# One tile of the second output projection interleaved with the last pair of stick-breaking heads, and four remainders computed on GpSimd

## The chip, the cores and the metric

One core of one Trainium2 chip runs the whole program. The metric is the device time of one execution in microseconds. The kernel before takes 3147.85 us, the median of three runs that lie between 3146.23 and 3148.41 us.

## What is computed

The program is two transformer blocks on 1024 positions of width 1024. What matters here is the attention part of the second block:

```
q, k, v, q_mem = split(x @ w_in_sb_2)                # 12 heads of 64 columns, and 4 memory heads
for each block of 128 queries:                       # stick-breaking attention
    z        = q_b @ k_b^T / 8
    log_stay = where(strict, log_sigmoid(-z), 0)
    later    = reverse_cumsum(log_stay) - log_stay
    w        = where(strict, exp(log_sigmoid(z) + later), 0)
    out      = w @ v_b
y = concat(mix, mem_out) @ w_out_2                   # the second output projection, 1024 x 1024
x = layer_norm(ALPHA * x + y)
```

The 12 stick-breaking heads give 768 rows of the projection's input, which are the blocks k = 0 to 5 of 128 rows (two heads in each). The memory attention gives the blocks 6 and 7 and is done before the stick-breaking stage.

## The kernel before

Activations lie transposed, features on the partitions. A dense layer is a series of tiles: one tile makes 128 output rows by 1024 positions in PSUM (`dense`, two slots, the use number u chooses u % 2), from 8 blocks of 128 input rows. Precision comes from a split: a value is the sum of a rounded part (`_hi`) and a remainder (`_lo`). One block of a tile is therefore six matmuls of 512 columns (`product`, L517, L518, L521: hi by hi and hi by lo for the two halves of the positions, then lo by hi for the two halves).

**Weights.** SyncE streams raw weight tiles into a ring of two. GpSimd splits each: one addition of zero into `w_hi` (L426), one subtraction into `w_lo` (L428), again a ring of two. The split of tile t waits until tile t - 2 is done (`pool.wait_ge(tile_done, t - 1)`), and a tile's first matmul waits for `weights_split`. In the stick-breaking stage GpSimd does the same work in four parts of 512 columns (`split_part`, L459 and L466), one part for a step, at the steps listed in `SPLIT_W`.

**The stick-breaking stage** is written out by hand in 144 steps: 12 for a head, 24 for a pair of heads, numbered n from 0. The last pair has steps 120 to 143. One step is a strip of 128 queries by up to 512 keys. In step n
- TensorE computes the scores of strip n (L934 to L936), transposes the weights of strip n - 6 (`turn_weights`, L946) and multiplies those of strip n - 8 by the values (`values`, L960 and L961); then it does two blocks of the next pair's projection, if `PROJECT` lists the step (the last one it lists is n = 125).
- ScalarE makes sigmoid(z) and sigmoid(-z) of strip n (L1378, L1384) and rounds the transposed weights of strip n - 6 (L1392). Its waits are for the scores and for `pv_done` of strip n - 7, less one.
- VectorE does the scan over strip n (L1935, preceded by a one-column product L1934 for the strips that go on from others, which are the last four of a head), then the remainder `wt_lo` of strip n - 6 (L1942), which reads PSUM. At n % 12 = 0 and 8 it also finishes a half head into `y2_f` (L1924; the page calls it y_f).
- GpSimd multiplies strip n by the scan (L476), then does its part of a weight split, if any.

TensorE starts the transposes of a step only when `w_split`, VectorE's remainder of two strips earlier, is there. So each engine runs ahead of the others by a step or so at most, and all work goes in the order in which it is written.

**The second output projection** has the tiles T_OUT2 (159) to T_OUT2 + 7. Its input blocks are taken in the order `Y2_ORDER` = 0, 1, 2, 3, 4, 6, 7, 5. Block 5 holds the last pair of heads and comes last. The first seven are made ready inside the stick-breaking loop: at the steps in `EARLY_AT`, which are n = 130, 132, ..., 142, ScalarE rounds `y2_f` into `a_hi` (L1406) and VectorE subtracts to make `a_lo` (the helper `low`, L1543). Block 5 follows after the loop. The weights of T_OUT2 are split at the steps 120 to 123, those of T_OUT2 + 1 at the steps 127 to 130.

After the loop TensorE waits for all heads (`y_copied`) and runs `two_tiles`: tile 0 and tile 1 of this projection together, tile 1 four blocks behind tile 0, so that tile 0 ends four blocks ahead of tile 1. Tile 0 uses slot 1 of `dense` (where the stick-breaking stage collects its outputs), tile 1 uses slot 0 (where it projects). The tiles 2 to 5 follow one by one, and `last_two` does the rest with the layer norm's sums. VectorE adds each tile to the residual (`add_mixed`, L1964) and adds up moments (L1481, L1471). ScalarE fetches the spilled residual from memory with two transfers that it issues once `y_copied` is complete (L1408, L1409).

Of the kernel before, what the change touches and what calls it, by code (L numbers as in the profile page):

```python
# [20 lines left out]
F32 = mybir.dt.float32  # L21
F32R = mybir.dt.float32r
ACT = mybir.ActivationFunctionType
ALU = mybir.AluOpType
# [5 lines left out]
KB = D // P  # L30
# [8 lines left out]
SB_H = 12  # L39
# [40 lines left out]
U_OUT2 = U_SB  # L80
# [53 lines left out]
           for c, a in enumerate((0, 7, 15)) for q in range(4) if p < SB_H // 2 or c < 2}  # L134
Y2_ORDER = (0, 1, 2, 3, 4, 6, 7, 5)
EARLY = 7
EARLY_AT = {PAIR_STEPS * (SB_H // 2 - 1) + 10 + 2 * j: j for j in range(EARLY)}


NORM_SPLIT = (None, 2, 0, 2, 4)  # L140
# [47 lines left out]
def build(nc, io, out):  # L188
    with ExitStack() as ctx:
# [5 lines left out]
        def sem(name):  # L195
            return ctx.enter_context(nc.semaphore(name))
# [69 lines left out]
        def par(name, k=0):  # L266
# [34 lines left out]
        parts = {n: (sem(n + "_rounded"), sem(n + "_split")) for n in (  # L301
            "h", "mem", "ym", "yc", "ya", "merged", "h2", "hidden", "x2", "mem2", "y2", "x3", "hidden2")}
        yc_ready = sem("conv_out_ready")

        turned, roped, turn_free = sem("proj_turned"), sem("proj_rotated"), pair("turn_free")
        idx_round, idx_split, stacked, stack_copied = (sem("index_rounded"), sem("index_split"), sem("index_stacked"),
# [116 lines left out]
        def _(pool):  # L423
# [48 lines left out]
            def stick_steps():  # L472
                for n in range(STICK_STEPS):
                    w, width = weights_of(n), chunk(n)[5]
                    pool.wait_ge(scanned, n + 1)
                    pool.tensor_tensor(w[:, 0:width - 1], w[:, 0:width - 1], stay[n % STRIPS][:, 1:width], ALU.mult  # L476
                                       ).then_inc(w_ready, 1)
                    if n in SPLIT_W:
                        t, part = SPLIT_W[n]
                        split_part(T_SB + t, part)  # L480

            split_tiles(RAW, T_ATT + 2)

# [17 lines left out]
        def _(pe):  # L501
# [467 lines left out]
            for n in range(STICK_STEPS + PV_LAG):  # L969
                if n < STICK_STEPS:  # L970
                    scores(n)
                if TURN_LAG <= n < STICK_STEPS + TURN_LAG:
                    turn_weights(n - TURN_LAG)
                if n >= PV_LAG:
                    values(n - PV_LAG)
                if n in PROJECT and PROJECT[n][0] < SB_H // 2:
                    p, c, half, b = PROJECT[n]
                    project(p, c, half, b, b + 2)
                if n in TURN_V:
                    turn_values(*TURN_V[n])  # L980

            pe.wait_ge(v_split, SB_H)
            pe.wait_ge(y_copied, 2 * SB_H)
            for n in range(KB):
                if n == 0:
                    two_tiles(T_OUT2, U_OUT2, parts["y2"][1], Y2_ORDER)
                elif 2 <= n < KB - 2:
                    tile(T_OUT2 + n, U_OUT2 + n)
            last_two(3, T_OUT2 + KB - 2, U_OUT2 + KB - 2, lambda h: moments(3, h, U_OUT2))
            repeat(pe, FF2_GROUPS - 1, feed(  # L990
                T_FF2, U_FF2, FG, parts["hidden2"][1], FG, (FF2_TILES, FF2_USES),
# [470 lines left out]
        def _(dve):  # L1462
# [455 lines left out]
            for n in range(STICK_STEPS + PV_LAG + 1):  # L1918
                e = n - PV_LAG - 1
                if e >= 0 and group_end(e) is not None:  # L1920

                    head, th = group_end(e) // 2, group_end(e) % 2
                    dve.wait_ge(low_ready, group_end(e) + 1)
                    dve.tensor_tensor(y2_f[HD * (head % 2):HD * (head % 2) + HD, head // 2, 512 * th:512 * th + 512],  # L1924
                                      out_bank(th)[0:HD, :], out_low[:, th, :], ALU.add).then_inc(y_copied, 1)
                if n < STICK_STEPS:
                    _, kind, _, _, _, width = chunk(n)
                    strip, before = stay[n % STRIPS], stay[(n - 4) % STRIPS]
                    dve.wait_ge(stay_ready, n + 1)
                    if kind == 2:  # L1930

                        dve.wait_ge(scanned, n - 3)
                        w = weights_of(n)
                        dve.tensor_tensor(w[:, 511:512], w[:, 511:512], before[:, 0:1], ALU.mult)  # L1934
                    dve.tensor_tensor_scan(strip[:, 0:width][:, ::-1], strip[:, 0:width][:, ::-1],  # L1935
                                           zero[:, 0:1].broadcast_to([P, width]), before[:, 0:1] if kind == 2 else 1.0,
                                           ALU.mult, ALU.add).then_inc(scanned, 1)
                m = n - TURN_LAG
                if 0 <= m < STICK_STEPS:
                    c0 = P * (3 - m % 4) if m % HEAD_STEPS < 8 else 0  # L1940
                    dve.wait_ge(w_round, m + 1)
                    dve.tensor_tensor(wt_lo[:, m % 2, c0:512], turn_bank(m, c0), wt_hi[:, m % 2, c0:512].bitcast(F32),  # L1942
                                      ALU.subtract).then_inc(w_split, 1)
                if n in TAKE_Q:
                    take_q(*TAKE_Q[n])
                if n in TAKE_K:
                    take_k(*TAKE_K[n])
                if n in SPLIT_V:
                    take_values(*SPLIT_V[n])
                if n in EARLY_AT:  # L1950
                    j = EARLY_AT[n]
                    k = Y2_ORDER[j]
                    low((a_hi[:, k, :], a_lo[:, k, :]), k, y2_f[:, k, :], "y2", j + 1)

            for j in range(EARLY, KB):
                k = Y2_ORDER[j]
# [272 lines left out]
```

## Time and profile before

| | us |
|---|---|
| median of three runs | 3147.85 |
| lowest and highest run | 3146.23, 3148.41 |
| the profiled execution's own time | 3153.3 |
| its span | 3151.5 |
| its mean granted TensorE clock | 0.96 of full speed |

The page gives for the span: PE 94% busy, weight loads 76%, VectorE 54%, ScalarE 25%, GpSimd 37%. In the page's table of 40 slices of 78.8 us, the last heads and the start of the projection lie in slices 29 and 30 (from 2206 us to 2364 us), where TensorE's digits are 7 and 9 and VectorE's 9 and 3. The granted clock is in tenths of full speed. Times below are microseconds from the start of the span; in the timelines the columns are start, duration, engine, line, operation, operands, and in brackets the idle time before with what ended it.

### The profile page before, as it was taken

The numbers are of one execution on the slowest core, as the hardware profiler recorded it, in microseconds if no ns is written. First come the engines' busy times: TensorE is split into PE (matmuls) and PEld (weight loads), VectorE is DVE, ScalarE is ACT, GpSimd is POOL, SyncE is SP. The second block draws the span as 40 slices with busy tenths as digits, with TensorE's granted clock in tenths as the row PEclk, the third lists the DMA queues.
The fourth block names the chain that finished last, engine by engine and source line by source line (L and its number), as shares of the span: only waits on it lengthen the run. The fifth ranks groups of instructions, "written<-read, shape, count | busy, mean of one in ns | idle before, by whom it ended". The sixth has DMA issues, their size and how long they took to land.

```text
span 3151.5 us, 35444 instructions
## 1 busy us (share of the span) xinstructions
PE 2962.3 (94%) x13362; PEld 2385.4 (76%) x13362; DVE 1690.4 (54%) x2322; ACT 781.9 (25%) x1429; POOL 1160.1 (37%) x649
## 2 busy tenths in 40 slices
PE   7987999998999899999999889999798999999997
PEld 4675878885777688888888668887675888888885
DVE  3475899985553533232332647888937333333327
ACT  4154011103531211011110355666613000000003
POOL 2330434441023334333443415555532433344331
PEclk9978999996999999999999999999898999999998
DMA  3110112221032111111111210000020111111111
GB/s 144 41 34 7 47 67 81 80 80 67 1 130 71 41 47 47 47 53 47 47 47 49 72 67 27 27 21 27 21 87 27 47 51 49 47 47 47 53 47 61
DMA packets 45054, 165.41 MB, mean 52 GB/s; under 512 B 4880, under 2 KB 6160, under 8 KB 43920
## 3 DMA queue, kind: packets, MB, share of 16 engines
q1 hardware_dynamic: 37168, 129.31, 12.4%
q10 hardware_dynamic: 7776, 34.61, 2.8%
q8 instruction: 72, 1.18, 0.2%
q14 instruction: 38, 0.31, 0.0%
HBM read 147.12 MB, written 16.78 MB: 52 GB/s over the span
## 4 chain that ended last, share of the span: by engine, by line
PE 82%; DVE 12%; ACT 2%; issue 2%; DVEq 1%; DMA 0%; POOL 0%; ACTq 0%; SPq 0%; POOLq 0%
PE dense L517 21%; PE dense L518 20%; PE dense L521 20%; DVE a_lo L1543 2%; DVE stay L1935 2%; PE dense L908 2%; PE side L813 2%; PE dense L909 2%; PE dense L910 2%; PE dense L557 1%; PE dense L823 1%; PE dense L558 1%; PE dense L559 1%; PE dense L740 1%; PE side L946 1%
## 5 line engine op out<-in xcount | busy, mean ns | idle before, releaser
L426 POOL TENSOR_TENSOR w_hi<-raw,zero 128x1024 fp32r<-128x1024 f32 x210 | 400.8, 1908 | 1572.2 <-PE dense L521 1300.2
L517 PE MATMUL dense<-a_hi,w_hi 128*128 128x512 f32 x2000 | 783.4, 392 | 14.1 <-DVE T L1681 5.6
L518 PE MATMUL dense<-a_lo,w_hi 128*128 128x512 f32 x2000 | 780.4, 390 | 0.0
L521 PE MATMUL dense<-a_hi,w_lo 128*128 128x512 f32 x2000 | 617.9, 390 | 0.0
L428 POOL TENSOR_TENSOR w_lo<-raw,w_hi 128x1024 fp32r<-128x1024 f32 x210 | 526.4, 2506 | 16.5
L517 PEld LDWEIGHTS dense<-a_hi,w_hi 128*128 128x128 f32 x2000 | 376.7, 188 | 95.7 <-issue 7.7
L521 PEld LDWEIGHTS dense<-a_hi,w_lo 128*128 128x128 f32 x2000 | 376.9, 188 | 78.9
L518 PEld LDWEIGHTS dense<-a_lo,w_hi 128*128 128x128 f32 x2000 | 376.7, 188 | 79.0 <-issue 1.2
L517 PE MATMUL dense<-b_hi,w_hi 128*128 128x512 f32 x832 | 327.2, 393 | 5.2 <-DVE T L1841 2.5
L518 PE MATMUL dense<-b_lo,w_hi 128*128 128x512 f32 x832 | 324.7, 390 | 0.0
L1821 DVE TENSOR_TENSOR x_res<-x_res,dense 128x1024 f32<-128x1024 f32 x100 | 122.1, 1221 | 329.6 <-PE dense L521 328.3
L1841 DVE SCALAR_TENSOR_TENSOR T<-dense,tiny,T 128x1023 f32<-128x1023 f32 x88 | 112.9, 1283 | 296.6 <-ACT T L1275 293.0
L521 PE MATMUL dense<-b_hi,w_lo 128*128 128x512 f32 x832 | 256.7, 390 | 0.0
L476 POOL TENSOR_TENSOR stick_weights<-stick_weights,stay 128x511 f32<-128x511 f32 (+2 forms) x144 | 132.1, 918 | 174.8 <-DVE stay L1935 174.8
L517 PEld LDWEIGHTS dense<-b_hi,w_hi 128*128 128x128 f32 x832 | 156.7, 188 | 45.8 <-issue 4.8
L1435 ACT ACTIVATE b_hi<-T 128x1024 fp32r<-128x1024 f32 x32 | 34.0, 1063 | 610.1 <-DVE T L2014 610.1
L521 PEld LDWEIGHTS dense<-b_hi,w_lo 128*128 128x128 f32 x832 | 156.5, 188 | 32.9
L518 PEld LDWEIGHTS dense<-b_lo,w_hi 128*128 128x128 f32 x832 | 156.8, 188 | 31.7
L1275 ACT ACTIVATE T<-dense,tiny 128x1024 f32<-128x1024 f32 x44 | 49.2, 1118 | 516.9 <-PE dense L521 511.1
L1646 DVE MATCH_REPLACE8 score<-tiny,score 128x384 f32<-128x384 f32 (+2 forms) x192 | 165.7, 878 | 0.0
L1642 DVE MAX8 tiny<-score 128x8 f32<-128x384 f32 (+2 forms) x192 | 155.4, 878 | 4.1 <-issue 3.1
L2012 DVE TENSOR_SCALAR T<-dense 128x1024 f32<-128x1024 f32 x32 | 39.2, 1225 | 191.5 <-PE dense L521 190.5
(263 smaller groups left out, 4405.6 us busy)
## 6 DMA issues: line engine op xcount, KB each, us to landing
raw<-in_w_stream SPq DMA_DIRECT2D x231, 512.0 KB, 3.4
x_in<-in_x_t SPq DMA_DIRECT2D x8, 512.0 KB, 7.3
spill_gate<-T ACTq DMA_DIRECT2D x8, 512.0 KB, 2.6
spill_part<-gates ACTq DMA_DIRECT2D x8, 512.0 KB, 2.7
back<-spill_gate ACTq DMA_DIRECT2D x8, 512.0 KB, 3.7
back<-spill_part ACTq DMA_DIRECT2D x8, 512.0 KB, 4.7
x_res<-in_x_t ACTq DMA_DIRECT2D x2, 2048.0 KB, 9.0
spill_x<-x_res ACTq DMA_DIRECT2D x1, 4096.0 KB, 13.5
```

The lines of the kernel that those rows point to most:

```text
L426: pool.tensor_tensor(w_hi[:, r % 2, :], raw[:, r, :], zero[:, 0:1].broadcast_to([P, D]), ALU.add).then_inc(weights_rounded, 1)
L428: pool.tensor_tensor(w_lo[:, r % 2, :], raw[:, r, :], w_hi[:, r % 2, :].bitcast(F32), ALU.subtract).then_inc(weights_split, 1)
L476: pool.tensor_tensor(w[:, 0:width - 1], w[:, 0:width - 1], stay[n % STRIPS][:, 1:width], ALU.mult).then_inc(w_ready, 1)
L517: pe.matmul(o, w_hi[:, slot, w], hi[:, k, x], start=b == 0, stop=False)
L518: pe.matmul(o, w_hi[:, slot, w], lo[:, k, x], start=False, stop=False)
L521: last = pe.matmul(o, w_lo[:, slot, w], hi[:, k, x], start=False, stop=stop)
L813: last = pe.matmul(side[:, n % 2, c:e], q_f[r, h % 3, i * P:i * P + P], k_f[r, c:e], start=True, stop=True)
L908: pe.matmul(o, w_hi[:, t % 2, w], a_hi[:, b, x], start=b == 0, stop=False)
L1642: dve.max(best[:, i - TOPK // P, :], score[:, score_at(i):score_at(i + 1)])
L1646: dve.match_replace(sc, best[:, i - TOPK // P, :], sc, TAKEN)
L1821: dve.tensor_tensor(x_res[:, n, :], x_res[:, n, :], dense[:, u % 2, :], ALU.add).then_inc(sums_free[u % 2], 1)
L1841: last = dve.scalar_tensor_tensor(T[:, slot, d:S], dense[:, u % 2, 0:S - d], tap, T[:, slot, d:S], ALU.mult, ALU.add)
```

## The change

Three things are done.

1. The rounding of the seven early input blocks moves three steps ahead, from n = 130, 132, ..., 142 to n = 127, 129, ..., 139.
2. Of their remainders, those with an even number j = 0, 2, 4, 6 are made by GpSimd at the end of its step (steps 127, 131, 135, 139), with a semaphore of their own, `y2_low`. VectorE keeps j = 1, 3, 5 (steps 129, 133, 137) and the last one after the loop.
3. TensorE does one block of tile T_OUT2 + 1 at the end of each of the steps n = 130, 132, ..., 142 (`FIRST_AT`), ahead of the scores of step n + 1. The first of them waits for the split of that tile's weights. After the loop it does seven blocks of tile T_OUT2, then the eighth block of T_OUT2 and of T_OUT2 + 1, then the other tiles as before.

```diff
-EARLY_AT = {PAIR_STEPS * (SB_H // 2 - 1) + 10 + 2 * j: j for j in range(EARLY)}
+EARLY_AT = {PAIR_STEPS * (SB_H // 2 - 1) + 7 + 2 * j: j for j in range(EARLY)}
+FIRST_AT = {n + 3: j for n, j in EARLY_AT.items()}
...
+        y2_low = sem("y2_split_by_pool")
...
                     if n in SPLIT_W:
                         t, part = SPLIT_W[n]
                         split_part(T_SB + t, part)
+                    if n in EARLY_AT and EARLY_AT[n] % 2 == 0:
+                        j, k = EARLY_AT[n], Y2_ORDER[EARLY_AT[n]]
+                        pool.wait_ge(parts["y2"][0], j + 1)
+                        pool.tensor_tensor(a_lo[:, k, :], y2_f[:, k, :], a_hi[:, k, :].bitcast(F32), ALU.subtract
+                                           ).then_inc(y2_low, 1)
...
                 if n in TURN_V:
                     turn_values(*TURN_V[n])
-
-            pe.wait_ge(v_split, SB_H)
+                if n in FIRST_AT:
+                    j = FIRST_AT[n]
+                    if j == 0:
+                        pe.wait_ge(v_split, SB_H)
+                        pe.wait_ge(weights_split, T_OUT2 + 2)
+                    pe.wait_ge(parts["y2"][1] if j % 2 else y2_low, j // 2 + 1)
+                    product((T_OUT2 + 1) % 2, halves(dense, (U_OUT2 + 1) % 2), a_hi, a_lo, j + 1, begin=j, end=False, order=Y2_ORDER)
+
             pe.wait_ge(y_copied, 2 * SB_H)
-            for n in range(KB):
-                if n == 0:
-                    two_tiles(T_OUT2, U_OUT2, parts["y2"][1], Y2_ORDER)
-                elif 2 <= n < KB - 2:
-                    tile(T_OUT2 + n, U_OUT2 + n)
+            product(T_OUT2 % 2, halves(dense, U_OUT2 % 2), a_hi, a_lo, EARLY, end=False, order=Y2_ORDER)
+            pe.wait_ge(parts["y2"][1], KB // 2)
+            for n in range(2):
+                product((T_OUT2 + n) % 2, halves(dense, (U_OUT2 + n) % 2), a_hi, a_lo, KB, begin=EARLY, order=Y2_ORDER
+                        ).then_inc(tile_done, 1)
+            for n in range(2, KB - 2):
+                tile(T_OUT2 + n, U_OUT2 + n)
...
                 if n in EARLY_AT:
                     j = EARLY_AT[n]
                     k = Y2_ORDER[j]
-                    low((a_hi[:, k, :], a_lo[:, k, :]), k, y2_f[:, k, :], "y2", j + 1)
+                    if j % 2:
+                        low((a_hi[:, k, :], a_lo[:, k, :]), k, y2_f[:, k, :], "y2", j + 1)
```

## Rows read from the trace of the kernel before

**Rows 1.** The page: the span, and busy time by engine

```profile
span 3151.5 us, 35444 instructions
PE 2962.3 (94%) x13362; PEld 2385.4 (76%) x13362; DVE 1690.4 (54%) x2322; ACT 781.9 (25%) x1429; POOL 1160.1 (37%) x649
```

**Rows 2.** Busy time by window; columns PE, PEld, DVE, ACT, POOL, clock, DMA, GB/s

```profile
2250.90:2259.00 8.10, 5.31 (x22) 4.57 (x21) 8.10 (x8) 3.44 (x7) 4.75 (x4) 0.50 0.20 65
2259.00:2269.20 10.20, 6.00 (x37) 4.72 (x37) 10.20 (x14) 8.29 (x18) 3.63 (x5) 1.00 0.01 2
...
2280.50:2289.70 9.20, 6.68 (x28) 5.68 (x28) 6.15 (x8) 2.17 (x5) 3.09 (x2) 0.50 0.00 0
```

**Rows 3.** Waits from 2240 to 2296 us: total, times, longest

```profile
PE side L946 <- DVE wt_lo L1942: 19.1, 14, 2.6
DVE wt_lo L1942 <- ACT wt_hi L1392: 4.5, 5, 1.3
```

**Rows 4.** VectorE's timeline, steps 128 to 143

```profile
2241.95 1.28 DVE L1935 TENSOR_TENSOR_SCAN stay<-stay,stay,zero 128x512 f32<-128x512 f32 x1
...
2246.52 0.66 DVE L1942 TENSOR_TENSOR wt_lo<-side,wt_hi 128x512 fp32r<-128x512 f32 x1
...
2247.71 2.38 DVE L1935 TENSOR_TENSOR_SCAN stay<-stay,stay,zero 128x512 f32<-128x512 f32 x1
...
2253.41 1.27 DVE L1935 TENSOR_TENSOR_SCAN stay<-stay,stay,zero 128x512 f32<-128x512 f32 x1
...
2263.25 0.41 DVE L1935 TENSOR_TENSOR_SCAN stay<-stay,zero 128x128 f32<-128x128 f32 x1
...
2280.34 1.21 DVE L1543 TENSOR_TENSOR a_lo<-y_f,a_hi 128x1024 fp32r<-128x1024 f32 x1
...
2282.44 1.27 DVE L1935 TENSOR_TENSOR_SCAN stay<-stay,stay,zero 128x512 f32<-128x512 f32 x1
```

**Rows 5.** VectorE's remainders between 2240 and 2296 us: count, busy time, mean ns

```profile
L1543 DVE TENSOR_TENSOR a_lo<-y_f,a_hi 128x1024 fp32r<-128x1024 f32 x7 | 11.9, 1693 | 0.0
```

**Rows 6.** TensorE's timeline at steps 130 and 131

```profile
2244.14 0.34 PE L961 MATMUL dense<-wt_lo,sv 128*128 128x384 f32 x1
2244.31 0.40 PE L935 MATMUL side<-ks,qs_hi 128*128 128x512 f32 x1
2244.54 0.40 PE L936 MATMUL side<-ks,qs_lo 128*128 128x512 f32 x1
```

**Rows 7.** GpSimd's timeline: steps 127 and 129 to 130, and the split after the loop

```profile
2240.91 1.04 POOL L459 TENSOR_TENSOR w_hi<-raw,zero 128x512 fp32r<-128x512 f32 x1
...
2247.73 1.28 POOL L466 TENSOR_TENSOR w_lo<-raw,w_hi 128x512 fp32r<-128x512 f32 x1
...
2251.22 2.25 POOL L466 TENSOR_TENSOR w_lo<-raw,w_hi 128x512 fp32r<-128x512 f32 x1
...
2312.43 1.90 POOL L426 TENSOR_TENSOR w_hi<-raw,zero 128x1024 fp32r<-128x1024 f32 x1 [27.55 <-PE dense L521]
2314.40 2.40 POOL L428 TENSOR_TENSOR w_lo<-raw,w_hi 128x1024 fp32r<-128x1024 f32 x1
...
2321.29 3.26 POOL L428 TENSOR_TENSOR w_lo<-raw,w_hi 128x1024 fp32r<-128x1024 f32 x1
```

**Rows 8.** ScalarE's timeline at step 131, and one rounding

```profile
2244.74 1.05 ACT L1406 ACTIVATE a_hi<-y_f 128x1024 fp32r<-128x1024 f32 x1
2245.69 0.59 ACT L1378 ACTIVATE stick_weights<-side 128x512 f32<-128x512 f32 x1
2246.17 0.60 ACT L1384 ACTIVATE stay<-side 128x512 f32<-128x512 f32 x1
```

**Rows 9.** TensorE's timeline after the loop: first matmul, slow ones, two blocks' ends

```profile
2295.51 0.47 PE L517 MATMUL dense<-a_hi,w_hi 128*128 128x512 f32 x1 [1.45 <-issue]
...
2297.75 0.63 PE L518 MATMUL dense<-a_lo,w_hi 128*128 128x512 f32 x1
2298.18 0.63 PE L517 MATMUL dense<-a_hi,w_hi 128*128 128x512 f32 x1
...
2314.45 0.61 PE L521 MATMUL dense<-a_hi,w_lo 128*128 128x512 f32 x2
...
2315.81 0.61 PE L521 MATMUL dense<-a_hi,w_lo 128*128 128x512 f32 x2
```

**Rows 10.** VectorE adds tile 0 and tile 1 to the residual

```profile
2312.45 1.22 DVE L1964 SCALAR_TENSOR_TENSOR x_res<-x_res,dense 128x1024 f32<-128x1024 f32 x1 [13.82 <-PE dense L521]
2319.18 1.22 DVE L1964 SCALAR_TENSOR_TENSOR x_res<-x_res,dense 128x1024 f32<-128x1024 f32 x1 [5.51 <-PE dense L521]
```

## The prediction

> **What bounds the kernel now.** I read the page first: TensorE is busy for 94% of the span [rows 1], so matmuls that are merely moved gain only if they land in time in which TensorE stands idle. Then I read the stretch that the change touches, in windows. In the last steps of the stick-breaking loop VectorE is busy without a gap: 8.10 of 8.10 us and 10.20 of 10.20 us, while TensorE has 5.31 and 6.00 [rows 2]. The waits say the same: from 2240 to 2296 us TensorE waits 14 times, 19.1 us in all, for VectorE's remainder of the transposed weights, and VectorE waits for ScalarE only 4.5 us, in the drain after the last scan [rows 3]. So the loop's last 18 steps are set by VectorE, and the 35 us behind it, up to the end of tile 1, by TensorE alone. The idea of the change fits: TensorE has some 19 us idle and VectorE carries seven remainders of 11.9 us [rows 5].
>
> Last I laid the engines' timelines side by side at step 130, because the new block there waits for the second tile's weights. TensorE is done with step 130 at about 2244.5 us [rows 6]; GpSimd ends the last part of that split, in its own step 130, at 2251.22 + 2.25 = 2253.47 us [rows 7]. TensorE runs some 9 us ahead of GpSimd at this place.
>
> **The change part by part**, against the span of 3151.5 us.
>
> *Blocks leave the end.* Behind the loop TensorE did 16 blocks and now does 9. A block takes 2315.81 - 2314.45 = 1.36 us at full clock [rows 9]. 7 x 1.36 = **-9.5 us**, all of it on the path. The last input block (rounding and remainder after `y_copied`) had ten blocks of cover and now has seven, 9.5 us; those two instructions take about 2.3 us (1.05 and 1.21) [rows 4, 8], so it stays hidden. The residual's transfers are issued as before; the first tile now ends about 12 us behind the loop instead of 16.9 (2312.45 - 2295.51) [rows 9, 10]. Nothing is charged: the first, smaller transfer has most of that time.
>
> *The next weights are exposed.* GpSimd may split tile 2's weights only when tile 0 is done. That takes from 2312.43 to 2314.40 + 2.40 = 2316.80, 4.4 us [rows 7], and with VectorE in its way the subtraction is 3.26 instead of 2.40. Before, tile 1 still had five blocks to go, 6.7 us (2319.18 - 2312.45) [rows 10], which hid it. Now tile 1 ends one block, 1.36 us, behind tile 0. TensorE stands idle for 4.4 + 0.1 - 1.36 = **+3.1 us** (+4.0 with the long subtraction; up to 1.5 more if the clock falls and a few matmuls start at 0.43 us apart as 2297.75 to 2298.18) [rows 9]. Tile 3's split then follows at once and lies under tile 2.
>
> *The wait at step 130.* Behind the waiting block stand, in TensorE's order, the scores of step 131, its transposes and its values. ScalarE needs those scores, VectorE needs ScalarE's sigmoid. Before, the scores of 131 were made at 2244.3 [rows 6], the sigmoids ended at 2246.8 [rows 8] and the scan began at 2253.41 [rows 4], so 6.6 us of lead are there to be used up. Now, from 2253.47: the block, 1.37 us at full clock or 6 x 0.43 = 2.6 at half; two score matmuls, 0.5 or 0.9; about 0.15 to ScalarE; its two sigmoids, 1.1. The scan of 131 starts at 2256.6 to 2258.2, which is +3.2 to +4.8 against 2253.41. TensorE has stood idle 9 us by then, and after much shorter gaps the trace shows the clock at 0.50 [rows 2], the 1.2 GHz level. I take +4.5 us.
>
> *GpSimd's remainder at step 127* is queued ahead of three of the four parts of this very split. A remainder is a subtraction of 128 x 1024, like the weights' one: 2.40 us [rows 7]. The trace shows what the two engines do to each other: VectorE's scan of 512 columns takes 1.27 us alone and 2.38 when GpSimd's subtraction of 1.28 us starts with it (2247.71 in rows 4, 2247.73 in rows 7), while the remainder from PSUM keeps its 0.66 us [rows 4]; and GpSimd's next one takes 2.25 instead of 1.28 [rows 7]. So the two exclude each other nearly for an instruction's length. The scan of 128 (2241.95) will be caught by the new subtraction, which can start at 2240.91 + 1.04 = 2241.95 [rows 7] and holds it until 2244.3. ScalarE's rounding, moved from step 130 to 127, costs the same scan up to 1.05 us [rows 8] beside this. VectorE's own remainder j = 1 comes in step 129 (1.2 to 1.7) where none was. Against that the one of step 130 is gone, but TensorE's wait would have hidden it anyway. Together they put the end of the split, and so all that follows, later by between 0 and 3.6 us. I take +2.3 us.
>
> *Refilling.* Step 131 starts with every queue empty and TensorE at half clock, with a second block at step 132. From there to step 135 I lay out the chain and find that VectorE stands idle once more for a scan, before step 133: **+1.5 us** (-1 to +3). Sum for the scan of step 135: about +8.3.
>
> *VectorE's relief afterwards.* From step 135 on the old kernel needs 2282.44 - 2263.25 = 19.2 us to the last scan [rows 4]. Three remainders leave (3 x 1.21 = 3.6 at the length without contention in rows 4; 5.1 at the mean of 1.69 in rows 5). Two of GpSimd's, at steps 135 and 139, come in, and each blocks a scan for up to 2.40 less the 0.66 us that VectorE can spend on its PSUM remainder: 2 x 1.7 = 3.4. TensorE's blocks of 1.36 us lie mostly in its idle time. Net **-0.5 us** (-4 to +1). The Trainium skill, page "SBUF — State Buffer", section "Who interferes with whom", has the rule behind this: VectorE with two SBUF inputs and GpSimd reading SBUF share one port pair, and whoever starts first blocks the other for the whole instruction. The trace agrees (1.27 becomes 2.38). By the rule the move to GpSimd is nearly a wash; without it the four would simply leave VectorE and this term would be -3.6 to -5.1.
>
> *The drain* from the last scan to the first matmul behind the loop takes 13.1 us (2282.44 in rows 4, 2295.51 in rows 9), most of it at clock 0.50 [rows 2]. More matmuls just before may keep the clock up: **-1 us** (0 to -2).
>
> Sum: -9.5 + 3.1 + 4.5 + 2.3 + 1.5 - 0.5 - 1 = +0.4 us, so a span near 3152. The profiled execution (3153.3) lies 5.4 us above the median of the runs, 3147.85, so the forecast for the median is 3148.3 us. All low ends together give -9.5 + 3.1 + 3.2 + 0 - 1 - 4 - 2 = -10.2, all high ones -9.5 + 5.5 + 4.8 + 3.6 + 3 + 1 = +8.4.
>
> **The rivals.** A measurement of this kernel can tell about 0.2%, 6.3 us, from no change; that bound is meant below.
>
> (A) *Faster.* The blocks fill idle time as meant, the stall at step 130 costs little more than its 3.2 us because the rest of VectorE's queue catches up, the removed remainders come off VectorE at full worth, and the drain runs at full clock: -9.5 + 3.1 + 3.2 - 4 - 2 = about -9 us, 3139 us. For it: VectorE is at 10.20 of 10.20 us [rows 2] and anything taken from it shows. Against it: the lock between the engines, and 9 us of waiting at step 130 that the order of the code makes certain.
>
> (B) *Slower.* The lead is never won back. From step 131 on TensorE's blocks stand between the values of one step and the scores of the next, and so in the ring TensorE, ScalarE, VectorE, TensorE. Of the six later blocks (6 x 1.36 = 8.2 us, more at half clock) all are then paid in the ring although they were moved away from the end: +0.4 + 8.2 = about +8.6, 3156.5 us. It decides when the ring's two-step length (transposes and values 0.9, block 1.36, scores 0.6, ScalarE's three instructions 1.7, hand-overs 0.3: 4.9 us) exceeds VectorE's two steps (19.2 / 8 x 2 = 4.8 us before, less what leaves it). The two are so near that I cannot exclude it; against it stand TensorE's idle gaps of up to 2.6 us before the transposes [rows 3], which a block must fill first.
>
> **How the numbers follow.** The forecast, a change too small to measure, 0.61; (A) 0.16; (B) 0.23. (B) gets more than (A) because the stall is certain and my terms behind it are gross, whereas (A) needs several low ends at once. The predicted time is the forecast's, 3148.3. The range reaches to both rivals: 3139.5 to 3157. Faster by over 0.2% is 0.16, within it 0.61, slower 0.23; the forecast's own range is 3142 to 3154.
>
> **What the changed profile would show.** Right: one wait of TensorE of 7 to 12 us before its first new block, released by GpSimd's L466; VectorE idle 4 us or more before the scan of step 131, which comes 6 to 8 us late; the clock near 0.5 there; an idle gap of 3 to 4 us before tile 2, ended by GpSimd's L428; 9 blocks instead of 16 behind the loop; scans stretched by a GpSimd subtraction of 2.4 us at steps 128, 132, 136, 140. Wrong towards (A): the first matmul behind the loop comes less than 3 us late. Wrong towards (B): it comes over 11 us late, and VectorE waits for ScalarE's sigmoid at every second step.

## The result, and the profile after

The changed kernel takes 3153.91 us, the median of 17 runs, against 3148.34 us for 17 runs of the kernel before: a ratio of 1.0018 with a 95% interval of 1.0011 to 1.0026. It is slower by 0.18%, just inside the 0.2% that I had called no change, and inside the range 3139.5 to 3157; the forecast was 3148.3 us. The interval excludes an unchanged time. Medians here and below leave out the executions recorded as slow, one of the five-block kernel's twelve (8113.52 us) and one of the kernel before in each comparison with an experiment.

The page of the changed kernel, span and busy time by engine (against [rows 1]):

```profile
span 3154.7 us, 35442 instructions
PE 2959.9 (94%) x13362; PEld 2382.7 (76%) x13362; DVE 1689.6 (54%) x2318; ACT 780.3 (25%) x1429; POOL 1167.9 (37%) x653
```

Nothing changed in bulk: four instructions moved from VectorE to GpSimd. What changed is the order, and that is read from the last pair of heads. What lies ahead of it differs by some microseconds from one execution to the next, so from here on every position is given as a distance from the start of the scan of step 120, the first of the last pair. That scan, in the kernel before and in the changed one (VectorE's timelines):

```profile
2223.84 1.23 DVE L1935 TENSOR_TENSOR_SCAN stay<-stay,zero 128x512 f32<-128x512 f32 x1
```

```profile
2223.70 1.23 DVE L1950 TENSOR_TENSOR_SCAN stay<-stay,zero 128x512 f32<-128x512 f32 x1
```

The marks, read in the same way from each kernel's timelines ("first matmul" is the first one behind the loop; the last column is the start of the addition of tile 2 to the residual, the point from which before and after run alike, 821.4 and 821.3 us to the end):

| us from the scan of step 120 | scan 131 | scan 135 | scan 143 | first matmul | tile 2 added |
|---|---|---|---|---|---|
| before | 29.57 | 39.41 | 58.60 | 71.67 | 106.29 |
| changed | 36.86 | 47.81 | 66.64 | 79.83 | 109.75 |
| difference | +7.29 | +8.40 | +8.04 | +8.16 | +3.46 |

So the loop loses 8.2 us and the stretch behind it gives back 4.7. Most of the loss, 7.3 us, is there at step 131. TensorE's timeline of the changed kernel shows where; the duration is the second column, the idle time before an instruction and what ended it stand in brackets:

```profile
2246.51 0.52 PE L968 MATMUL dense<-wt_lo,sv 128*128 128x384 f32 x1
2255.79 0.77 PE L524 MATMUL dense<-a_hi,w_hi 128*128 128x512 f32 x1 [8.76 <-issue]
2256.36 0.63 PE L525 MATMUL dense<-a_lo,w_hi 128*128 128x512 f32 x1
...
2258.49 0.60 PE L942 MATMUL side<-ks,qs_hi 128*128 128x512 f32 x1
...
2320.76 0.77 PE L524 MATMUL dense<-a_hi,w_hi 128*128 128x512 f32 x1 [3.19 <-POOL w_lo L430]
```

TensorE is done with step 130 and then stands still for 8.76 us. The profile puts this down to "issue", since it finds no releaser; GpSimd's timeline does, because the last part of the weights' split ends at 2254.43 + 1.26 = 2255.69 us, 0.1 us before the block starts:

```profile
2241.78 2.37 POOL L486 TENSOR_TENSOR a_lo<-y_f,a_hi 128x1024 fp32r<-128x1024 f32 x1
...
2254.43 1.26 POOL L468 TENSOR_TENSOR w_lo<-raw,w_hi 128x512 fp32r<-128x512 f32 x1
...
2316.30 1.89 POOL L428 TENSOR_TENSOR w_hi<-raw,zero 128x1024 fp32r<-128x1024 f32 x1 [22.67 <-PE dense L528]
2318.27 2.34 POOL L430 TENSOR_TENSOR w_lo<-raw,w_hi 128x1024 fp32r<-128x1024 f32 x1
```

The block's matmuls start 0.43 us apart, the half clock, and only then come the scores of step 131 (2258.49). VectorE's timeline shows the other end of the chain, and what GpSimd's new instructions do to it:

```profile
2242.68 1.48 DVE L1949 TENSOR_TENSOR stick_weights<-stick_weights,stay 128x1 f32<-128x1 f32 x1 [0.43 <-ACT stay L1399]
...
2260.48 0.16 DVE L1949 TENSOR_TENSOR stick_weights<-stick_weights,stay 128x1 f32<-128x1 f32 x1 [6.99 <-ACT stay L1399]
2260.56 1.28 DVE L1950 TENSOR_TENSOR_SCAN stay<-stay,stay,zero 128x512 f32<-128x512 f32 x1
...
2263.43 2.97 DVE L1950 TENSOR_TENSOR_SCAN stay<-stay,zero 128x512 f32<-128x512 f32 x1 [0.43 <-ACT stay L1399]
...
2273.20 2.72 DVE L1950 TENSOR_TENSOR_SCAN stay<-stay,zero 128x512 f32<-128x512 f32 x1 [0.62 <-ACT stay L1399]
```

VectorE, which has no gap at this place in the kernel before, is idle 6.99 us. And a product of a single column, 0.16 us by itself, takes 1.48 us at step 128: it ends at 2244.16, exactly when GpSimd's remainder does (2241.78 + 2.37 = 2244.15). The scans of 132 and 136 take 2.97 and 2.72 us, where they took 1.41 and 1.21 before, for the same reason; at step 140 it is the product again (1.25 us).

The last scan is stretched too, not by a remainder but by GpSimd's product for the strip before, which begins with it. In the kernel before this scan took 1.27 us [rows 4]:

```profile
2290.34 2.12 DVE L1950 TENSOR_TENSOR_SCAN stay<-stay,stay,zero 128x512 f32<-128x512 f32 x1
```

```profile
2290.25 1.12 POOL L478 TENSOR_TENSOR stick_weights<-stick_weights,stay 128x511 f32<-128x511 f32 x1 [1.29 <-DVE stay L1950]
```

Behind the loop TensorE has nine blocks. GpSimd starts on tile 2's weights at 2316.30, when tile 0 is done, and ends at 2320.61; tile 2 waits 3.19 us for it and starts at half clock. VectorE's additions, tiles 0 and 1 in one row and then tile 2 (against [rows 10]):

```profile
2316.33 2.51 DVE L1980 SCALAR_TENSOR_TENSOR x_res<-x_res,dense 128x1024 f32<-128x1024 f32 x2 [9.63 <-PE dense L528]
...
2333.45 1.22 DVE L1980 SCALAR_TENSOR_TENSOR x_res<-x_res,dense 128x1024 f32<-128x1024 f32 x1 [11.74 <-PE dense L528]
```

### The profile page after: what moved, and what is told of

It is laid out like the page before. It is cut to its first block, busy times and chain, and to the rows that moved or that the text cites. A ratio compares the mean times of both kernels' runs of the same rounds, so it can differ in the third digit from the quotient of the medians.

```text
span 3154.7 us, 35442 instructions
## 1 busy us (share of the span) xinstructions
PE 2959.9 (94%) x13362; PEld 2382.7 (76%) x13362; DVE 1689.6 (54%) x2318; ACT 780.3 (25%) x1429; POOL 1167.9 (37%) x653
## 4 chain that ended last, share of the span: by engine, by line
PE 82%; DVE 11%; issue 3%; ACT 3%; DVEq 1%; DMA 0%; POOL 0%; ACTq 0%; SPq 0%; POOLq 0%
PE dense L524 20%; PE dense L525 20%; PE dense L528 20%; PE dense L915 2%; PE side L820 2%; DVE stay L1950 2%; PE dense L916 2%; PE dense L917 2%; DVE a_lo L1558 1%; PE dense L564 1%; PE dense L830 1%; PE dense L565 1%; PE dense L566 1%; PE dense L747 1%; PE side L953 1%
```

## The experiments

My theory: the loop loses by TensorE's wait at step 130, with the scores of step 131 queued behind it; the blocks themselves run in idle time; a remainder on GpSimd costs VectorE what it takes off it. The rivals: the blocks lengthen the ring of engines wherever they stand, and GpSimd does relieve VectorE. Each edit is against the changed kernel unless it says otherwise, and is cut to the lines that matter. `BY_POOL` lists the remainders that GpSimd makes (0, 2, 4, 6 in the changed kernel), `FIRST_BLOCKS` the number of tile 1's blocks in the loop.

### The blocks three steps later

```diff
-FIRST_AT = {n + 3: j for n, j in EARLY_AT.items()}
+FIRST_AT = {n + 6: j for n, j in EARLY_AT.items() if j < 7}
```

> The changed kernel with TensorE's seven early blocks three steps later, at the ends of the steps 133, 135, ..., 145, so that the weights of the second tile are split before the first of them is due; the rest as changed. The changed kernel's scan of step 131 starts 7.1 us later than before, its first matmul behind the loop 8.0 us later, tile 2's eviction 3.3 us later. My theory (the wait at step 130 is what the loop loses): no such wait, the scan of 131 within 1 us of before, the first matmul behind the loop at +0 to +2 us, tile 2's eviction at -5 to -3 us, the time 3143 to 3146 us. Rival (the blocks themselves lengthen the ring of engines, wherever they stand): the first matmul behind the loop still at +4 us or more, the time 3149 or more.

Measured: 3144.54 us, ratio 0.9992 (0.9981 to 1.0002). Scan 131 at 29.75 us (+0.2), first matmul at 72.34 (+0.7), tile 2 added at 102.53 (-3.8). VectorE's timeline (steps 120 and 131) and TensorE's first matmul behind the loop:

```profile
2219.28 1.23 DVE L1956 TENSOR_TENSOR_SCAN stay<-stay,zero 128x512 f32<-128x512 f32 x1
...
2249.03 2.12 DVE L1956 TENSOR_TENSOR_SCAN stay<-stay,stay,zero 128x512 f32<-128x512 f32 x1
...
2291.62 0.56 PE L526 MATMUL dense<-a_hi,w_hi 128*128 128x512 f32 x1 [1.40 <-DVE y_f L1945]
```

One number moved by three steps takes 7.5 us out of the loop (79.83 to 72.34). The ring theory falls as the account of the 8 us: seven blocks stand in the loop, and it is under 1 us longer than before. Of that 0.7 the next kernels show that it is not the blocks' either.

### The wait by itself

On the kernel of the section "No early tile" below, with one wait added at the end of step 130 and no block there:

```diff
+                if n == PAIR_STEPS * (SB_H // 2 - 1) + 10:
+                    pe.wait_ge(v_split, SB_H)
+                    pe.wait_ge(weights_split, T_OUT2 + 2)
```

> The kernel no_early_tile (16 blocks behind the loop) with one wait added: TensorE waits at the end of step 130 for the second tile's weights, and does no block there. It measures the wait by itself. In no_early_tile the scan of step 131 starts 29.8 us behind that of step 120, in the changed kernel 36.9, of which one block at half clock is 2.6. Theory: the wait alone puts the scan of 131 at 34 to 34.8 us, the first matmul behind the loop at 77 to 78.5 (72.7 without the wait), tile 2's eviction at 112 to 113, the time 3154 to 3157. Rival (the wait is absorbed, the block or the clock makes the loss): scan of 131 at 32 or less, first matmul behind the loop at 74.5 or less, the time 3151 or less.

Measured: 3155.13 us, ratio 1.0030 (1.0020 to 1.0041). Scan 131 at 34.50 (29.76 without the wait), first matmul at 77.94 (72.68), tile 2 added at 112.49 (107.31). TensorE's first row after the wait, and VectorE's at step 131:

```profile
2255.60 0.77 PE L944 MATMUL side<-ks,qs_hi 128*128 128x512 f32 x1 [9.19 <-issue]
```

```profile
2257.95 0.16 DVE L1965 TENSOR_TENSOR stick_weights<-stick_weights,stay 128x1 f32<-128x1 f32 x1 [4.65 <-ACT stay L1415]
```

A wait of 9.19 us costs 4.7 us at scan 131 and 5.3 at the end of the loop; the rest is lead that was used up. The block behind the wait adds 36.86 - 34.50 = 2.36 us in the changed kernel. So the wait and the block in its place are 7.1 of the 7.3 us at scan 131.

### All remainders on VectorE

```diff
+BY_POOL = ()
...
-                    if n in EARLY_AT and EARLY_AT[n] % 2 == 0:
+                    if n in EARLY_AT and EARLY_AT[n] in BY_POOL:
...
-                    if j % 2:
+                    if j not in BY_POOL:
                         low((a_hi[:, k, :], a_lo[:, k, :]), k, y2_f[:, k, :], "y2", j + 1)
```

TensorE's waits follow VectorE's count for every block.

> The changed kernel with all seven early remainders on VectorE, at the changed steps; the early blocks as changed. My theory (a remainder on GpSimd costs VectorE by the exclusion nearly what it takes off it, and the one at step 127 delays the weights' split): the first new block starts 1 to 2.5 us earlier than in the changed kernel, the rest of the loop is within 2 us of it, the first matmul behind the loop at +5 to +8 us against before; the time 3150 to 3154. Rival (GpSimd does relieve VectorE): four remainders of 1.2 to 1.7 us come back on VectorE's path, the first matmul behind the loop at +11 or more, the time 3157 or more.

Measured: 3148.37 us, ratio 1.0001 (0.9992 to 1.0010). First matmul at 78.08, which is 1.75 us sooner than in the changed kernel: taking four instructions back onto VectorE makes it faster. The relief theory falls. But my own expectation missed too: the time is below the 3150 to 3154 us that I gave, and the first new block starts only 0.35 us earlier (31.74 against 32.09), not 1 to 2.5. The split of the weights is late with either engine, so it is not GpSimd's remainder at step 127 that delays it, as I had put it, but that rounding and remainders come three steps earlier, by whomever they are made.

### No early tile

The changed kernel with the old order of 16 blocks behind the loop (tile 1 four blocks behind tile 0) and none in it:

```diff
-FIRST_AT = {n + 3: j for n, j in EARLY_AT.items()}
+FIRST_AT = {n + 3: j for n, j in EARLY_AT.items() if j < 0}
```

> Only the first two parts of the change: rounding three steps earlier and four remainders on GpSimd; TensorE's tiles in the order of before, 16 blocks behind the loop. My theory: no wait at step 130, and the moved remainders are nearly a wash: the first matmul behind the loop at -1.5 to +1.5 us against before, no idle time before tile 2, the time 3147 to 3150. Rival (relief of VectorE is worth its removed 4.8 to 6.8 us): first matmul behind the loop at -4 us or less, the time 3144 or less.

Measured: 3150.68 us, ratio 1.0009 (1.0000 to 1.0018), a little above what I expected. Scan 131 at 29.76, scan 143 at 59.48, first matmul at 72.68 (+1.0), tile 2 added at 107.31 (+1.0). Against the late blocks (29.75, 59.54, 72.34) the loop is the same to 0.06 us up to its last scan, with five blocks ahead of that scan in the one and none in the other: **blocks in TensorE's idle time are free here** (one of them is not in the kernel with the old steps, below). Busy time in 18 us from 40 us behind the scan of step 120, no early tile and then late blocks (columns as in [rows 2]):

```profile
2261.60:2279.60 18.00, 11.76 (x53) 9.03 (x53) 18.00 (x21) 12.84 (x27) 14.43 (x11) 0.74 0.00 0
```

```profile
2259.28:2277.28 18.00, 13.14 (x72) 10.23 (x72) 18.00 (x21) 12.62 (x26) 14.43 (x11) 1.00 0.00 0
```

VectorE is busy 18.00 of 18 us in both. The blocks raise the granted clock from 0.74 to 1.00, and even that buys nothing in a stretch that VectorE sets.

### Five blocks instead of seven

```diff
-FIRST_AT = {n + 3: j for n, j in EARLY_AT.items()}
+FIRST_AT = {n + 3: j for n, j in EARLY_AT.items() if j < 5}
+FIRST_BLOCKS = 5
...
-                product((T_OUT2 + n) % 2, halves(dense, (U_OUT2 + n) % 2), a_hi, a_lo, KB, begin=EARLY, order=Y2_ORDER
+                product((T_OUT2 + n) % 2, halves(dense, (U_OUT2 + n) % 2), a_hi, a_lo, KB, begin=FIRST_BLOCKS if n else EARLY, order=Y2_ORDER
```

> The changed kernel with only the first five of the early blocks in the loop; tile 1 has three blocks to do behind tile 0's end. My theory (the split of tile 2's weights, 4.4 us, is exposed, and TensorE's clock falls in that wait): 11 blocks behind the loop, idle time before tile 2 of under 1 us instead of 3.2, no half clock behind it, so tile 2's eviction 1 to 2 us earlier than in the changed kernel though two blocks more stand behind the loop; the loop as changed within 1 us. The time 3151.5 to 3153.5. Rival (each block in the loop costs its 1.36 us there): the loop ends 2.7 us earlier, the time 3149 to 3151. If the exposure were worth nothing, tile 2's eviction would come 2.7 us later.

Measured: 3150.34 us, ratio 1.0009 (1.0000 to 1.0018). From first matmul to tile 2 added it takes 28.51 us instead of 29.92, 1.4 us less with two blocks more, as expected. But tile 2 is not added earlier (110.03 against 109.75), for the loop is a miss: its first matmul comes at 81.51, 1.7 us later than in the changed kernel, though it holds two blocks less. Up to step 139 the two kernels are the same instructions, and yet the scan of 139 stands at 58.60 against 56.94. The clock differs between them. Nine microseconds of each at the same distance from the scan of step 120 (from 41.7), five blocks and then the changed kernel:

```profile
2259.70:2268.70 9.00, 7.14 (x33) 6.23 (x34) 7.57 (x9) 4.60 (x10) 3.44 (x6) 0.81 0.00 0
```

```profile
2265.40:2274.40 9.00, 6.80 (x39) 5.76 (x40) 8.38 (x10) 5.17 (x11) 4.91 (x5) 1.00 0.00 0
```

Behind the stall VectorE has no work in hand and waits (7.57 of 9.00 us busy), so a stretch of half clock is paid there in full. That this is the whole of the 1.7 us is argued, not shown.

### Late blocks with all remainders on VectorE, and with the old steps

The first of these, late_on_vector, is the late blocks (`n + 6`) with the remainders on VectorE, the second, late_old_steps, has in addition the old `EARLY_AT`, so the blocks stay at the steps 133 to 145:

```diff
-EARLY_AT = {PAIR_STEPS * (SB_H // 2 - 1) + 7 + 2 * j: j for j in range(EARLY)}
-FIRST_AT = {n + 3: j for n, j in EARLY_AT.items()}
+EARLY_AT = {PAIR_STEPS * (SB_H // 2 - 1) + 10 + 2 * j: j for j in range(EARLY)}
+FIRST_AT = {n + 3: j for n, j in EARLY_AT.items() if j < 7}
+BY_POOL = ()
```

> Blocks three steps later and all seven remainders on VectorE, rounding at the changed steps 127 to 139. Distances here are from the start of the scan of step 120, since what lies ahead of the loop's last pair differs by some us from one execution to the next: the first matmul behind the loop stood at 71.7 us before, 79.8 changed, 72.3 with late blocks alone; tile 2's eviction at 106.3, 109.8, 102.5. My theory (a remainder on GpSimd costs VectorE nearly what it takes off it, or a little more): first matmul behind the loop at 70.5 to 72.5 us, tile 2's eviction 100.7 to 102.7, the time 3142 to 3145. Rival (GpSimd relieves VectorE once no wait hides it): first matmul behind the loop at 74 or more, the time 3146 or more.

> The kernel before with nothing but the early tile: rounding and remainders at the steps 130 to 142 and on VectorE as before, the seven blocks at the ends of the steps 133 to 145. Theory (blocks in TensorE's idle time cost the loop nothing): first matmul behind the loop at 71.2 to 71.9 us from the scan of step 120 (71.7 before), tile 2's eviction at 101.2 to 102.0 (106.3 before), the time 3142.5 to 3144.5. Against late_on_vector it tells what the three steps' move of rounding costs by itself: I expect up to 1 us. Rival (the ring pays for blocks): first matmul at 73 or more.

Measured: 3143.22 us, ratio 0.9988 (0.9979 to 0.9997), first matmul at 70.42, tile 2 added at 98.99; and 3144.64 us, ratio 0.9993 (0.9983 to 1.0003), 71.47 and 101.21. With the late blocks above, this takes the change apart one part at a time, at the first matmul behind the loop. The drain is the stretch from the start of the last scan to that matmul:

| step | scan 143 | drain | first matmul, us | difference |
|---|---|---|---|---|
| before | 58.60 | 13.07 | 71.67 | |
| seven blocks at 133 to 145 | 59.54 | 11.93 | 71.47 | -0.20 |
| rounding and remainders three steps earlier | 57.62 | 12.80 | 70.42 | -1.05 |
| four remainders to GpSimd | 59.54 | 12.80 | 72.34 | +1.92 |
| blocks three steps earlier (the wait) | 66.64 | 13.19 | 79.83 | +7.49 |

Two of the small differences are sums of larger ones. The seven blocks cost the old loop 0.94 us up to its last scan and give back 1.14 in the drain. The cost starts at step 136, whose scan comes 0.80 us later than before (41.13 against 40.33). TensorE's and VectorE's timelines of the kernel with the old steps:

```profile
2259.75 0.39 PE L526 MATMUL dense<-a_hi,w_hi 128*128 128x512 f32 x1
...
2261.20 0.45 PE L944 MATMUL side<-ks,qs_hi 128*128 128x512 f32 x1
```

```profile
2263.03 1.23 DVE L1956 TENSOR_TENSOR_SCAN stay<-stay,zero 128x512 f32<-128x512 f32 x1 [0.74 <-ACT stay L1405]
```

The same scores in TensorE's timeline of the kernel before:

```profile
2261.76 0.44 PE L935 MATMUL side<-ks,qs_hi 128*128 128x512 f32 x1
```

The block of step 135 stands ahead of the scores of step 136 and puts them 1.38 us later (39.30 us from the scan of step 120 against 37.92), and VectorE then waits 0.74 us for ScalarE's sigmoid of them. So the ring theory does hold for this one block, at 0.8 us. The move of rounding and remainders gains 1.92 us up to the last scan and loses 0.87 in the drain, because the last scan is stretched from 1.27 to 2.12 us in every kernel that has the move.

The first expectation was too high by 1.7 us at tile 2, because I had taken the half clock at the first blocks behind the loop for fixed; in this kernel it is not there (tile 0 is added 11.28 us behind the first matmul, 12.87 with the late blocks). So of the 3.5 us between the two kernels at tile 2 the remainders explain 1.9, and this clock 1.6.

### Placing five blocks

Three more kernels have five blocks in the loop and all remainders on VectorE. The first, late_old_five, has the steps of before (blocks at 133 to 141), the others round at 127 to 139 and place the blocks later, the second, five_spread, as here and the third, five_drain, two steps later still:

```diff
-FIRST_AT = {n + 3: j for n, j in EARLY_AT.items()}
+FIRST_AT = {137: 0, 139: 1, 141: 2, 143: 3, 145: 4}
```

> As late_old_steps, with only the first five blocks in the loop (steps 133 to 141), so that tile 1 covers the split of tile 2's weights. Between first matmul behind the loop and tile 2's eviction the changed kernel took 29.9 us and the one with five blocks 28.5, before 34.6. Expected: the loop as in late_old_steps within 0.5 us, tile 2's eviction 1.4 us earlier than there, at 99.8 to 100.6 us from the scan of step 120, the time 3141 to 3143.5, which would be below both kernels. Rival (the loop's drain needs the last blocks to keep the clock up): the first matmul behind the loop 1 us or more later, which eats the gain.

> late_on_vector (rounding at the steps 127 to 139, all remainders on VectorE) with five blocks of tile 1 in the loop, at the ends of the steps 137, 139, ..., 145, late enough to fill TensorE's gaps just ahead of the drain. Distances from the scan of step 120: late_on_vector had its first matmul behind the loop at 70.4 us and tile 2's eviction at 99.0; late_old_five, whose clock fell to half in the drain, had 72.4 and 101.1. Theory: the clock stays at 1.00 through the drain as with seven blocks, the first matmul behind the loop at 70.2 to 71.2, 11 blocks behind it with at most 0.5 us of idle time, tile 2's eviction at 97 to 98.3, the time 3139 to 3142, the fastest of all. Rival (fewer blocks, clock at half in the drain or at the first blocks behind the loop): tile 2's eviction at 98.8 or later, the time no better than late_on_vector's 3143.

> As five_spread with the blocks two steps later, at the ends of the steps 139, 141, 143, 145, 147; the last one stands in the drain, where the engines work in turn with no slack. Theory: a block of 1.36 us at step 147 is paid there by 0.5 to 1.4 us unless TensorE waits longer than that; first matmul behind the loop at 70.8 to 72, tile 2's eviction at 97.5 to 99, the time 3140 to 3143. Rival (TensorE's gaps in the drain take it too): as five_spread within 0.3 us.

Measured: 3143.05 us, ratio 0.9981 (0.9971 to 0.9991), first matmul at 72.41, tile 2 at 101.07: its rival came true, nearly 1 us later than with seven blocks, and the gain of the shorter wait is eaten. Then 3140.61 us, ratio 0.9975 (0.9966 to 0.9984), 70.67 and 97.70; and 3140.79 us, ratio 0.9975 (0.9962 to 0.9987), 71.14 and 98.18, where the block at step 147 costs 0.5 us and the time cannot be told from the second's. The windows from the last scan to the first matmul, late_old_five (scan of 143 at 59.52), late_old_steps (59.54) and five_spread (57.88):

```profile
2273.48:2286.37 12.89, 8.03 (x34) 5.83 (x35) 6.97 (x11) 3.58 (x6) 1.15 (x2) 0.75 0.01 1
```

```profile
2281.44:2293.37 11.93, 7.81 (x45) 5.47 (x43) 6.98 (x11) 4.08 (x7) 1.15 (x2) 1.00 0.01 1
```

```profile
2279.49:2292.28 12.79, 8.35 (x48) 5.84 (x46) 7.81 (x12) 4.23 (x8) 2.12 (x2) 1.00 0.00 1
```

The first two kernels are alike up to their last scans (within 0.02 us) and both have it at 1.27 us; they differ in the blocks of the steps 143 and 145 and in the clock. At clock 1.00 the drain is 0.96 us shorter, though a block more stands in it. The third has the clock too, but its last scan takes 2.12 us and uses up 0.85 of it. Counted from the end of the last scan the drain takes 11.80 us at clock 0.75 (before), 11.62 at 0.78 (late_old_five), 11.07 at 0.84 (changed) and 10.66 to 10.68 at 1.00 (late_old_steps, late_blocks, late_on_vector, five_spread).

The first blocks behind the loop depend on the clock again: in the 8 us from the first matmul it is 0.79 in late_old_five, where tile 0 is added 85.31 - 72.41 = 12.90 us behind that matmul, and 1.00 in five_spread, where it is 81.94 - 70.67 = 11.27. A clock of 1.00 in the drain does not secure it: the late blocks had 1.00 there and 0.79 behind it. What decides it stays open. And tile 2 waits for its weights only this long, TensorE's timeline of five_spread:

```profile
2308.04 0.47 PE L526 MATMUL dense<-a_hi,w_hi 128*128 128x512 f32 x1 [0.51 <-POOL w_lo L432]
```

This version beats both kernels: 3140.61 us, 7.1 below the 3147.67 of before in the same comparison.

## Why the prediction was right

The forecast was a change too small to measure, with the loop losing what the end gains. The mechanism is what came, and the time lies inside the bound of 0.2%, but only just: it moved by 5.6 us where the sum had +0.4 and the bound is 6.3, and the interval, 0.11% to 0.26%, excludes no change and reaches past the bound. Two terms, the end and the drain, missed to the same side by 2.8 us together; that they did not miss by more is luck as much as skill. By the steps of its sum:

| step | predicted | measured | from |
|---|---|---|---|
| 7 blocks leave the end | -9.5 | -9.5 | counted: 16 blocks to 9, still 1.36 us each; with the next row it gives the 4.7 us measured |
| tile 2's weights exposed | +3.1 | +3.2 and +1.6 | idle time 3.19; half clock behind it |
| wait at 130, step 127's delay | +4.5, +2.3 | +7.3 | scan 131 |
| refilling to scan 135 | +1.5 | +1.1 | 8.40 - 7.29 |
| scan 135 to scan 143 | -0.5 | -0.4 | 8.04 - 8.40 |
| the drain | -1 | +0.1 | 8.16 - 8.04 |
| sum at tile 2 | +0.4 | +3.5 | |

- **The wait at step 130** was the right term and the right size. Its signs came as listed: a wait of 8.8 us where 7 to 12 was said, VectorE idle 6.99 us, the scan of 131 7.3 us late, scans of 132 and 136 stretched by a subtraction of 2.4 us (at 128 and 140, where I had said scans as well, it was the one-column product ahead of the scan). The wait-only kernel shows that the wait does 4.7 us of it and the block behind it the rest.
- **Step 127** was sized right and named wrong. The split ended 2.36 us later than before (31.99 against 29.63 from the scan of step 120), predicted +2.3. I ascribed most of it to GpSimd's remainder. With all of them on VectorE the block starts 0.35 us sooner, no more: it is the three steps' move. By itself, with no wait in its way, that move even gains 1.05 us at the first matmul.
- **VectorE's relief** held in its direction and size up to the last scan (-0.4 for -0.5), where the profile of before alone, with a busy VectorE, invites a gain of 4.8 us or more. But the four remainders on GpSimd are worse than a wash: against the same steps with all of them on VectorE they cost 1.9 us, and 1.75 behind the wait. The rule of the Trainium skill that was weighed there ("SBUF — State Buffer", "Who interferes with whom") agrees with the one-column product that ended together with GpSimd's subtraction, 1.48 us instead of 0.16.
- **What was mis-sized** is the end. The half clock behind the 3.19 us of idle time costs (2333.45 - 2320.76) less a tile at full clock and the hand-over (10.9 + 0.2), 1.6 us. I had it in the bounds as up to 1.5 and left it out of the sum. And I gave the drain 1 us for a better clock. It got the better clock (0.86 against 0.72 in the two windows below, before and changed), and from the end of the last scan it is 0.73 us shorter (11.80 to 11.07). What I had not seen is that the last scan would meet GpSimd's product and take 2.12 us instead of 1.27, which is 0.85 more: together the +0.1. The late blocks, with clock 1.00, show what the full clock is worth there, 1.1 us (11.80 to 10.68).

```profile
2282.44:2295.51 13.07, 8.77 (x35) 6.24 (x35) 6.97 (x11) 3.59 (x6) 1.15 (x2) 0.72 0.00 0
```

```profile
2290.34:2303.53 13.19, 8.68 (x39) 5.91 (x39) 7.82 (x12) 4.26 (x8) 2.13 (x2) 0.86 0.01 1
```

Rival (B) was right that the change loses more than my sum had, and wrong in its mechanism: nothing net is paid for the later six blocks, since from the scan of 131 to the first matmul the kernel with the wait and no block takes 43.44 us and the changed one 42.97. Where VectorE had not been held up first, the ring did charge 0.8 us for one block. Rival (A), -9 us, is not reached even without the wait: the late blocks alone give -3.8 us at tile 2, and with the remainders left on VectorE -7.3.

One thing stays open. The marks explain +3.5 us, the medians differ by 5.6, with an interval from 3.5 to 8.2 us. Over the other kernels the change of the median differs from that of the marks, which come from one profiled execution each, by -1.9 to +3.0 us, more often upwards, so the 2.1 us here are within that spread. The marks leave out what lies ahead of step 120, where all kernels have the same instructions and yet the scan of step 120 stands anywhere from 2213.96 to 2223.84 us, and what lies behind tile 2 (820.1 to 821.7 us). I have no cause for either. The twelve runs of late_old_five fall into two groups, five at 3134 to 3138 us and seven at 3142.9 to 3145.3, and the profiled one is of the first group; its scan of step 120 is the one at 2213.96, 4 us ahead of the next earliest. So for that kernel the marks say more than the median. The five-block kernel shows that behind the stall the same instructions can take 1.7 us more or less.

## What to carry to other kernels

Before a piece of work is put into an engine's idle time, read when its last operand is ready by the producer's timeline, not when the engine is free: work that waits in an in-order queue holds back everything behind it. Here the same seven blocks lose 7.5 us more when they begin at step 130 than when they begin three steps later. Even without a wait a block can stand ahead of another engine's input and cost part of its length (0.8 us of 1.4 at step 135). And when a stretch keeps its length though the clock in it rose, look for what else in it grew, before the clock is called worthless there: here it was one scan. Where work is taken from the end of a stage, ask what it was covering there (the next weights' split) and leave just that much behind; and count a move from VectorE to GpSimd as no relief while both read on-chip memory, until a run shows it.

## What the runs showed of the hardware that I had not expected

- The exclusion between VectorE and GpSimd holds for tiny instructions too: a one-column product of 0.16 us waited out GpSimd's subtraction and took 1.48 us. Its cost goes by the length of the instruction that holds the memory path, not by the one that wants it.
- Raising TensorE's granted clock from 0.74 to 1.00 for 18 us changed nothing measurable in a stretch set by VectorE (0.06 us at the last scan). In the drain, where three engines work in turn and TensorE is busy 8.03 of 12.89 us, 0.75 against 1.00 is worth 1.0 us (12.89 against 11.93), and at the first blocks behind the loop, where TensorE works without a gap, 0.79 against 1.00 over 8 us is worth 1.6.
- After the 3.19 us without a matmul behind nine blocks at full clock, tile 2's first matmuls of the changed kernel started at the lower level (0.43 us apart, 1.2 GHz). The four other kernels with that gap of 3.19 us did the same (late_blocks, late_on_vector, late_old_steps, remainders_on_vector). With 0.51 us of idle time at the same place, in five_spread, the next tile started at full clock.
